# The high half of each weight times both halves of the activation in one 512-column matmul

## The reference, cut to what matters

```
def conv_ffn(h, w_in, conv_w, conv_b, w_out):
    u = h @ w_in
    u = causal depthwise convolution of u along the tokens (3 taps) + conv_b
    a, g = jnp.split(u, 2, axis=-1)
    return (a * jax.nn.gelu(g, approximate=True)) @ w_out

for layer in range(DEPTH):
    mod = (silu(c) @ ada_w[layer] + ada_b[layer])          # 6 sections: shift, scale, gate, twice
    h = rms_norm(x, ...) * (1.0 + sc_m) + sh_m
    x = x + g_m * rms_norm(mixer(h), ...)
    h = rms_norm(x, ...) * (1.0 + sc_f) + sh_f
    x = x + g_f * rms_norm(conv_ffn(h, ...), ...)
```

## The kernel before

| phase | layer 0: units, pieces per unit | layer 1 |
|---|---|---|
| gates | 1, 0 | 1, 0 |
| columns | 16, 1.5 | 16, 1.5 (side work: decays) |
| values (function `tokens`) | 8, 1 | 16, 0 (side work: GLA) |
| columns | 8, 2 (side work: fox) | 16, 0 (side work: GLA) |
| values | 8, 2 (fox) | |
| columns | 8, 1 (mLSTM) | |
| mixed (output projection) | 16, 1.5 | 16, 1.5 |
| ff_up / ff_down, group 0 | 32, 1 / 16, 1.5 | 32, 1 / 16, 0 |
| ff_up / ff_down, group 1 | 32, 1 / 16, 1.5 | 32, 0 / 16, 0 |
| ff_up / ff_down, group 2 | 24, 1 / 16, 0.5 | 24, 0 / 16, 0 |

## Time and profile before

### The profile page before, as it was taken

How to read it: one execution, slowest core, us unless ns; L and a number is a source line. 1 busy time by engine, 2 the same in 40 slices (tenths; PEclk the granted TensorE clock), 3 DMA queues, 4 the chain that set the end, 5 groups by cost and what they waited for, 6 DMA issues and landing times.

```text
span 2725.8 us, 48585 instructions
## 1 busy us (share of the span) xinstructions
PE 2538.6 (93%) x19382; PEld 2460.2 (90%) x19382; DVE 2017.8 (74%) x1998; ACT 1076.9 (40%) x1111; POOL 460.7 (17%) x230
## 2 busy tenths in 40 slices
PE   2599998989999999999989999989999999999997
PEld 2498877979999999999988989989899999999997
DVE  7876876789977799688777676667999456645655
ACT  1333334454433333233455544444533334333444
POOL 0100000013420244013301000000344014411320
PEclk7699989989999999999999999989999999999998
DMA  9887764747768767787665644357477455445543
GB/s 394 319 312 272 276 229 147 264 184 263 277 250 309 266 256 276 269 296 261 239 232 215 236 152 151 143 207 272 175 270 265 169 185 185 180 177 183 185 172 137
DMA packets 114640, 630.38 MB, mean 231 GB/s; under 512 B 12736, under 2 KB 12864, under 8 KB 62928
## 3 DMA queue, kind: packets, MB, share of 16 engines
q1 hardware_dynamic: 114512, 628.57, 63.0%
HBM read 626.42 MB, written 2.10 MB: 231 GB/s over the span
## 4 chain that ended last, share of the span: by engine, by line
PE 79%; DVE 9%; DMA 6%; ACT 3%; issue 2%; POOL 0%; DVEq 0%; SPq 0%; ACTq 0%; POOLq 0%
PE bank L1437 23%; PE bank L1438 22%; PE bank L1439 22%; DMA piece<-ada_pieces 4%; DVE acc L820 3%; PE bank L1456 2%; PE bank L1458 2%; PE bank L1457 2%; PE bank L1263 2%; DMA region<-ada_pieces 2%; DVE lo L806 1%; ACT hi L440 1%; PE bank L1341 1%; DVE act L865 1%; PE bank L1256 1%
## 5 line engine op out<-in xcount | busy, mean ns | idle before, releaser
L440 ACT ACTIVATE hi<-raw 128x2048 fp32r<-128x2048 f32 x402 | 769.6, 1915 | 1365.4 <-PE bank L1439 1238.0
L1437 PE MATMUL bank<-act,hi 128*128 128x256 f32 x4384 | 1266.8, 289 | 42.3 <-DVE act L865 26.1
L1438 PE MATMUL bank<-act,hi 128*128 128x256 f32 x4384 | 1252.7, 286 | 0.0
L1439 PE MATMUL bank<-act,lo 128*128 128x256 f32 x4384 | 1252.4, 286 | 0.0
L806 DVE TENSOR_TENSOR lo<-raw,hi 128x2048 fp32r<-128x2048 f32 x402 | 920.2, 2289 | 186.6 <-ACT hi L440 185.4
L1437 PEld LDWEIGHTS bank<-act,hi 128*128 128x128 f32 x4384 | 854.5, 195 | 52.6 <-issue 37.6
L1438 PEld LDWEIGHTS bank<-act,hi 128*128 128x128 f32 x4384 | 854.9, 195 | 1.0
L1439 PEld LDWEIGHTS bank<-act,lo 128*128 128x128 f32 x4384 | 854.0, 195 | 0.0
L820 DVE SCALAR_TENSOR_TENSOR acc<-piece,cond,acc 128x1024 f32<-128x1024 f32 x300 | 436.9, 1458 | 84.3 <-DMA piece<-ada_pieces 83.7
L1437 PE MATMUL bank<-mid,hi 128*128 128x256 f32 x1408 | 408.7, 290 | 12.3 <-POOL mid L790 11.2
L1438 PE MATMUL bank<-mid,hi 128*128 128x256 f32 x1408 | 402.2, 286 | 0.0
(11 more groups left out here) (155 smaller groups left out, 1612.0 us busy)
## 6 DMA issues: line engine op xcount, KB each, us to landing
raw<-w_units SPq DMA_DIRECT2D x402, 1024.0 KB, 4.8
piece<-ada_pieces SPq DMA_DIRECT2D x320, 512.0 KB, 4.9
region<-ada_pieces SPq DMA_DIRECT2D x64, 512.0 KB, 8.6
x<-x_in SPq DMA_DIRECT2D x1, 2048.0 KB, 15.0
x_out<-x SPq DMA_DIRECT2D x4, 512.0 KB, 2.6
vec<-vectors SPq DMA_DIRECT2D x1, 542.5 KB, 3.7
extra<-blocks_in SPq DMA_DIRECT2D x1, 512.0 KB, 18.9
causal<-causal_in SPq DMA_DIRECT2D x1, 256.0 KB, 18.1
```

Of the source, the lines that this page charges most:

```text
L440: sc.activation(hi[:, slot, :], raw[:, raw_slot, :], ACT.Copy).then_inc(s_hi, 1)
L1437: pe.matmul(dst, w_hi, src[:, kt, 0:T], start=at == 0, stop=False)
L1438: pe.matmul(dst, w_hi, src[:, kt, T:2 * T], start=False, stop=False)
L1439: i_ = pe.matmul(dst, w_lo, src[:, kt, 0:T], start=False, stop=at == len(order) - 1)
```

## The change

For each K tile the two matmuls with the same stationary operand `w_hi` become one of 512 columns, whose moving operand is the high and low half of the activation side by side. It writes a whole bank: columns 0:T hold high times high, columns T:2T weight-high times activation-low. The third matmul adds to columns 0:T as before. The two halves have to be added when the tile is taken out. VectorE can read one operand from PSUM, so ScalarE first copies columns T:2T into a new SBUF tile `low` (`stage_low`, with a semaphore `s_low`), and VectorE adds it. There is one `low`, so ScalarE also waits until the tile before has been taken out. In `ff_up` VectorE forms the sum in `low` and the convolution's three steps read it there; in `ff_down` groups 1 and 2 it adds `y` to `low` and then the tile. `stage_low` is the last thing in ScalarE's body of a unit, so it stands ahead of `hi` of the unit after next. The phases of kind `values` are as they were. `ones` shrinks to make room.

```diff
+            def stage_low(ph, i, j):
+                t = ph.t0 + j
+                sc.wait_ge(s_unit, SPLIT_SLOTS + unit(ph, i, j) + 1)
+                sc.wait_ge(s_evac, 2 + t + i * ph.tiles)
+                sc.activation(low[:, :], bank[2 * (t % 2)][:, T:2 * T], ACT.Copy).then_inc(s_low, 1)
...
                         if ph.sums and not (first_body(i) and j == 0):
                             square_tile(ph, ph.units * i + j - 1, (j + 1) % 2)
+                        if ph.kind != "values" and not (ph.side == "mlstm" and j == 3):
+                            stage_low(ph, i, j)
...
-                        if ph.kind != "values" or j % 4 == 3:
+                        if ph.kind != "values":
+                            ve.wait_ge(s_low, ph.c0 + i * ph.units + j + 1)
+                        elif j % 4 == 3:
                             ve.wait_ge(s_unit, SPLIT_SLOTS + n + 1)
...
                         elif ph.kind == "columns":
-                            ve.tensor_copy(region[:, bass.ds((ph.dest + ph.units * i + j) * T, T)], tile_ps)\
+                            ve.tensor_tensor(region[:, bass.ds((ph.dest + ph.units * i + j) * T, T)], tile_ps, low[:, :],
+                                             ALU.add).then_inc(s_evac, 1)
...
                         elif ph.kind == "ff_down":
                             at_ = flat(y[:, bass.ds(4 * i + j, 1), :])
-                            ve.tensor_tensor(at_, at_, tile_ps, ALU.add).then_inc(s_evac, 1)
+                            ve.tensor_tensor(low[:, :], at_, low[:, :], ALU.add).then_inc(s_v, own.tick())
+                            mine()
+                            ve.tensor_tensor(at_, tile_ps, low[:, :], ALU.add).then_inc(s_evac, 1)
...
-                            ve.tensor_scalar(out_, tile_ps, vec[:, bass.ds(ch + 2, 1)], vec[:, bass.ds(ch + 3, 1)],
+                            ve.tensor_tensor(low[:, :], tile_ps, low[:, :], ALU.add).then_inc(s_v, own.tick())
+                            mine()
+                            ve.tensor_scalar(out_, low[:, :], vec[:, bass.ds(ch + 2, 1)], vec[:, bass.ds(ch + 3, 1)],
                                              ALU.mult, ALU.add).then_inc(s_v, own.tick())
                             mine()
-                            ve.scalar_tensor_tensor(out=out_[:, 1:T], in0=tile_ps[:, 0:T - 1],
+                            ve.scalar_tensor_tensor(out=out_[:, 1:T], in0=low[:, 0:T - 1],
...
-                            ve.scalar_tensor_tensor(out=out_[:, 2:T], in0=tile_ps[:, 0:T - 2],
+                            ve.scalar_tensor_tensor(out=out_[:, 2:T], in0=low[:, 0:T - 2],
...
-                    dst = bank[2 * ((ph.t0 + j) % 2)][:, 0:T]
+                    both = bank[2 * ((ph.t0 + j) % 2)][:, :]
...
-                        pe.matmul(dst, w_hi, src[:, kt, 0:T], start=at == 0, stop=False)
-                        pe.matmul(dst, w_hi, src[:, kt, T:2 * T], start=False, stop=False)
-                        i_ = pe.matmul(dst, w_lo, src[:, kt, 0:T], start=False, stop=at == len(order) - 1)
+                        pe.matmul(both, w_hi, src[:, kt, :], start=at == 0, stop=False)
+                        i_ = pe.matmul(both[:, 0:T], w_lo, src[:, kt, 0:T], start=False, stop=at == len(order) - 1)
```

More of the change, by code:

```diff
@@ L68, in __init__, with place @@
         self.peel = self.head = 0
-    def place(self, n, t, a, pairs):
-        self.n0, self.t0, self.a0, self.pairs = n, t, a, pairs
+    def place(self, n, t, a, pairs, c):
+        self.n0, self.t0, self.a0, self.pairs, self.c0 = n, t, a, pairs, c
         self.end = n + self.bodies * self.units
@@ L75, in place @@
         pairs += 2 * self.bodies if self.kind == "ff_up" else 0
-        return self.end, t + self.bodies * self.tiles, self.a_end, pairs
+        c += 0 if self.kind == "values" else self.bodies * self.units
+        return self.end, t + self.bodies * self.tiles, self.a_end, pairs, c
     def straight(self, i):
@@ L111, in plan @@
               Phase("ff_up", 1, 6, 4, no, 2), Phase("ff_down", 1, 4, 4, no, 2)]
-    state = (0, 0, 2 * PIECES, 0)
+    state = (0, 0, 2 * PIECES, 0, 0)
     for ph in phases:
@@ L139 @@
 REGION = V_AT + TB * D
-OWN = {("ff_up", None): 8, ("columns", "fox"): 6, ("values", "fox"): 12, ("columns", "mlstm"): 14,
+OWN = {("ff_up", None): 12, ("columns", "fox"): 6, ("values", "fox"): 12, ("columns", "mlstm"): 14,
        ("values", "gla"): 8, ("columns", "gla"): 8}
@@ L223, in program @@
         ident = sb("ident", [P, P])
-        ones = sb("ones", [P, T])
+        ones = sb("ones", [P, P])
+        low = sb("low", [P, T])
         causal = sb("causal", [P, TB, T])
@@ L303, in program @@
         s_evac = sem("tile_evacuated")
+        s_low = sem("low_product_staged")
         s_piece = [sem(f"piece_ready{j}") for j in range(ADA_SLOTS)]
@@ L896, in gate_rows_ready @@
                 ve.wait_ge(s["masks_ready"], 1)
-                ve.tensor_tensor_scan(gate_rows, ones[0:GATES, :], gate_t2, 0.0, ALU.mult, ALU.add)\
+                ve.tensor_tensor_scan(gate_rows, ones[0:GATES, 0:1].broadcast_to([GATES, T]), gate_t2, 0.0, ALU.mult, ALU.add)\
                   .then_inc(s_v, own.tick())
@@ L1183, in body @@
                             bias = vec[0:GATES, V_GATEB:V_GATEB + 1] if ph.layer == 0 else 0.0
-                            ve.tensor_scalar(gates[:, :], tile_ps[0:GATES], bias, None, ALU.add).then_inc(s_evac, 1)
+                            ve.scalar_tensor_tensor(out=gates[:, :], in0=tile_ps[0:GATES], scalar=bias, in1=low[0:GATES, :],
+                                                    op0=ALU.add, op1=ALU.add).then_inc(s_evac, 1)
                         elif ph.kind == "columns":
-                            ve.tensor_copy(region[:, bass.ds((ph.dest + ph.units * i + j) * T, T)], tile_ps)\
+                            ve.tensor_tensor(region[:, bass.ds((ph.dest + ph.units * i + j) * T, T)], tile_ps, low[:, :],
+                                             ALU.add).then_inc(s_evac, 1)
+                        elif ph.kind == "mixed" or (ph.kind == "ff_down" and ph.group == 0):
+                            ve.tensor_tensor(flat(y[:, bass.ds(4 * i + j, 1), :]), tile_ps, low[:, :], ALU.add)\
                               .then_inc(s_evac, 1)
-                        elif ph.kind == "mixed" or (ph.kind == "ff_down" and ph.group == 0):
-                            ve.tensor_copy(flat(y[:, bass.ds(4 * i + j, 1), :]), tile_ps).then_inc(s_evac, 1)
                         elif ph.kind == "ff_down":
                             at_ = flat(y[:, bass.ds(4 * i + j, 1), :])
-                            ve.tensor_tensor(at_, at_, tile_ps, ALU.add).then_inc(s_evac, 1)
+                            ve.tensor_tensor(low[:, :], at_, low[:, :], ALU.add).then_inc(s_v, own.tick())
+                            mine()
+                            ve.tensor_tensor(at_, tile_ps, low[:, :], ALU.add).then_inc(s_evac, 1)
                         elif ph.kind == "ff_up":
@@ L1214, in body @@
                         k += ph.ada[j]
-                per = OWN.get((ph.kind, ph.side), 0)
+                per = ph.units if ph.kind == "ff_down" and ph.group > 0 else OWN.get((ph.kind, ph.side), 0)
                 roots_per = 2 if ph.side == "mlstm" else 0
```

## The result

| | before | changed |
|---|---|---|
| median, four executions each on one chip | 2718.97 us | 2742.78 us |
| lowest, highest | 2718.3, 2723.91 | 2730.93, 2745.96 |
| span of the profiled execution | 2725.8 us | 2744.2 us |
| mean granted clock | 0.958 | 0.950 |

The ratio is 1.0077 [1.0055, 1.0099]: slower by 0.8%, where 2701 was forecast and 2730 was the upper end of the range. A later repeat gave 1.0086 [1.0055, 1.0117].

What follows compares the result with a forecast made beforehand. TensorE was taken to bound the kernel, with VectorE 5% behind in 120 of 402 units. Terms -27.4 - 9 - 1 + 10 + 10.5, written as -17.9, took 2718.6 to 2701 us; range 2670 to 2730.

Steps and rivals of the forecast that it cites:

- the length of the chain in `ff_up`: VectorE's four evacuation steps per tile in `ff_up` with pieces, claimed to take 1.94 us.
- 5.86: Unit time in us for `ff_up` with pieces: 5.39 of VectorE work plus 0.47 given to GpSimd; +10 in all.
- the dearer evacuation: Rival: VectorE's evacuation in `ff_up` costs more, GpSimd's product hitting its SBUF-fed steps; 6.26 us per unit, 2747 us; chance 0.14.
- Phases where TensorE stays the bound, -27.4: Layer 1's `ff_up` and `ff_down`, `ff_down` group 2 and GLA's `columns` gain from the shorter matmuls, staging hidden: -27.4 us.
- The slack of 0.85: Where TensorE stays the bound, `hi` then `lo` end 4.7 us after a unit's end, weights wanted at 5.55.
- The merged matmul's 0.2266: Time in us per 512-column matmul, taken from `tokens`, against 0.2404 for two of 256 columns.
- Phases with three pieces in two units, -9: First `columns`, both `mixed` and layer 0's `ff_down` groups 0 and 1, 96 units: -9 us, against -20.6 at full rate.
- the limit by transfers: In layer 0's `ff_down` group 0, once the raw slots drain, piece DMAs set 12.1 us per pair of units.
- Ends of phases, +10.5: Staging and sum lengthen the last tile's path at phase changes, and the change of heads in GLA's `columns`: +10.5 us.
- GpSimd once per unit, 0.47: In `ff_up` with pieces VectorE gives GpSimd about 0.47 us once per unit, on the piece after `lo`.
- The five terms: TensorE-bound phases -27.4, three-piece phases -9, small chains (`fox`, `mlstm`, `gates`) -1, `ff_up` with pieces +10, phase ends +10.5.

Runs made afterwards that it cites:

- e3: The changed kernel with VectorE's `ff_up` bodies written out straight instead of looped; 2710.58 us, 0.9952 of the kernel before.
- e4: The changed kernel with the 16 wide matmuls of every tile issued first, then the 16 narrow ones; 2753.24 us, 1.0115 of the kernel before.
- e2: The changed kernel with the wide matmul but the old evacuation, leaving weight-high times activation-low out of the result; 2675.47 us, 0.984 of the kernel before.
- e6: e3 with the wide matmuls first in all but the first unit of a phase; 2702.60 us, 0.9946 of the kernel before.

## Why the prediction was wrong

**The step that failed** is the length of the chain in `ff_up`: "the chain is 0.46 + 0.43 + 0.52 + 0.53 = 1.94". In the loop it measures 0.60 + 0.56 + 0.63 + 0.73 = 2.52 beside a GpSimd step and 0.61 + 0.56 + 0.63 + 0.40 = 2.20 in the other unit. The rows it rested on were true and were the wrong unit. Without GpSimd the chain is 0.26 us longer than forecast; the other terms came out 0.12 shorter together, and 5.86 became 6.0. The forecast also took some 112 units as alike. By an estimate, 76 looped ones at 6.0 instead of 5.76 make +18, the straight ones stay under 5.76, and +18.0 was measured. e3 gives the control: with the gaps gone the chain is 0.45 + 0.45 + 0.52 + 0.40 = 1.82, the unit 5.71, the phases 719.3. So 1.94 was too long even for a straight unit, since the last step takes 0.40 to the next start and not 0.53: two errors of opposite sign, of which the loop's was the larger.

**The rival that came true** is the dearer evacuation, with 2747 given for 6.26 us per unit and 6.0 as the point from which it decides. The total came near its figure through other parts: the unit is 6.0, and the phases where TensorE was to stay the bound gave too little. Its reason, an extra price of the product on the new steps, holds only in part (below).

**Phases where TensorE stays the bound, -27.4.** In layer 1's `ff_up` without pieces -12.0 was expected and -2.1 came. VectorE has no piece there, but its chain of 2.2 us in gaps pushes `lo` back. Timelines of the changed kernel, VectorE and then GpSimd:

```profile
2285.86 2.83 DVE L819 TENSOR_TENSOR lo<-raw,hi 128x2048 fp32r<-128x2048 f32 x1
```

```profile
2285.81 0.73 POOL L803 TENSOR_TENSOR mid<-region,mid 128x256 f32 x1 [2.68 <-ACT mid L696]
```

The split of `mid` starts 0.05 us before `lo`, and `lo` takes 2.83 in place of 2.28. One unit in four then takes 6.05 to 6.2 us on TensorE, where the others take 5.55 to 5.75. The slack of 0.85 that the forecast worked out was for `lo` behind `hi`; it left out a GpSimd step in front of `lo`. In e3 the meeting is gone, and -9.4 of -12.0 came. In `ff_down` layer 1 groups 0 and 1 it is -1.9 for -6.8 + 1.8, since 0.3531 us per K tile gives 5.65 per unit and not 5.55. The merged matmul's 0.2266 was right (0.228 to 0.229 in the regular stream of e4); that a wide and a narrow one in turn need not add up to 0.3467 no row of before could show.

**Phases with three pieces in two units, -9.** Read by the table with 1.8 + 0.9 for their ends, -6.3 was due and -3.9, +0.1 and -1.7 came, -5.5. The sum is near, the reason is not: layer 0's first `columns` was to gain nothing and gained 4.2 us, and in `ff_down` group 0 of layer 0 the limit by transfers didn't appear. ScalarE's timeline of the changed kernel, `hi` in that phase (as the earlier trace rows):

```profile
809.00 1.91 ACT L443 ACTIVATE hi<-raw 128x2048 fp32r<-128x2048 f32 x1
...
893.88 1.91 ACT L443 ACTIVATE hi<-raw 128x2048 fp32r<-128x2048 f32 x1
```

These are 15 steps in 84.88 us, 5.66 each, to the end; before they fell to 6.07 after eight units. A slower `ff_up` ahead of it (199.2 for 194.4 us) leaves more in reserve, which would fit, but the repeat of the same kernel speaks against it. There `ff_up` took 200.0 us and the limit is back, in the phase that then takes 97.8 us:

```profile
880.84 1.91 ACT L443 ACTIVATE hi<-raw 128x2048 fp32r<-128x2048 f32 x1
...
893.09 1.91 ACT L443 ACTIVATE hi<-raw 128x2048 fp32r<-128x2048 f32 x1
```

These two units take 12.25 us, after seven of 5.68. In e2, where `ff_up` is faster (190.7), it is there too:

```profile
836.39 1.93 ACT L440 ACTIVATE hi<-raw 128x2048 fp32r<-128x2048 f32 x1 [4.95 <-PE bank L1438]
...
848.92 1.93 ACT L440 ACTIVATE hi<-raw 128x2048 fp32r<-128x2048 f32 x1 [4.97 <-PE bank L1438]
```

There two units take 12.53 us (836.39 to 848.92) after seven of 5.54, and the phase is 96.4 as before (96.5). e6 has `ff_up` at 192.6 and no limit (91.1). So the limit comes and goes between executions of one program, the first profile happened not to show it, and what brings it on is not settled.

**Ends of phases, +10.5.** This was the best part. Waits of the changed kernel:

```profile
PE bank L1458 <- POOL mid L803: 15.1, 4, 5.5
```

TensorE's wait for the last `mid` went from 11.2 to 15.1 us in the four places that this row holds. The first units of the six `ff_down` phases, from first matmul to first matmul, went from 7.11 to 8.29, 7.27 to 8.29, 9.37 to 10.42, 7.32 to 8.03, 7.05 to 7.72 and 9.40 to 10.22: +5.4 together, and 5.4 was said. The change of heads in GLA's `columns` went from 10.64 to 13.14 us, +2.5 for +2. That phase ends 4.1 us above before where -1.4 was due: its steps gave only 1.7 of 3.4, and its last unit, up to the first matmul of the next phase, went from 15.76 to 19.07, +3.3 us for which the forecast had no term. e3 and the repeat have the same 19.1; in e2, without staging and sum, it is 13.99.

**GpSimd once per unit, 0.47.** Of the size, right: the piece takes 1.76 beside it and 1.28 alone in the rows above. Wrong was that it always falls on the piece. In `ff_up` with pieces GpSimd was already running when the piece's sum started 108 times before, and 62 times in the changed kernel; 10 times it was `lo` (2.83 for 2.28, as above) and 36 times L1229, as at 1013.51 with 0.81 for 0.48. GpSimd's timeline:

```profile
1013.30 0.74 POOL L803 TENSOR_TENSOR mid<-region,mid 128x256 f32 x1 [2.58 <-ACT mid L696]
```

The Trainium skill (SBUF — State Buffer, the section "Who interferes with whom") says that a VectorE instruction with two SBUF inputs contends with a GpSimd instruction that reads SBUF. By the same page of the Trainium skill, section "SBUF: two separate sides", the one that starts first has the ports for its whole instruction. The trace agrees at all three places, with 0.33 to 0.55 us each. Whether the sum into `low`, which has one SBUF input, would have been spared no row of the changed kernel shows: none of its 176 ran beside a GpSimd instruction. How much of the loss is the exclusion and how much the loop's gaps was not tried apart: a kernel with GpSimd's steps shortened wasn't run.

**The sum.** The five terms add up to -16.9, not the -17.9 written; the forecast should have read 2702. e3's span lies 17.0 below before, which looks like that forecast without the loops' gaps. It is luck: with pieces it has -4.7 for +10, elsewhere it falls short by about as much, and the spans differ by 4 us more than the medians do (-13.0 against before on the same chip).

| us | forecast, ends of phases included | changed - before |
|---|---|---|
| start | 0 | +0.4 |
| `ff_up` with pieces | +10 | +18.0 |
| `ff_up` without | -12.0 | -2.1 |
| `ff_down` layer 1, groups 0, 1 | -5.0 | -1.9 |
| `ff_down` group 2 | -1.6 | +1.1 |
| GLA `columns` | -1.4 | +4.1 |
| three pieces in two units | -6.3 | -5.5 |
| gates, values, fox, mLSTM | -0.6 | +4.1 |
| sum | -16.9 | +18.2 (span +18.4) |

The last row but one is not clear of what executions differ by (405.1, 403.6 in the repeat, 399.0 in e3), and the lower granted clock in the fox `columns` goes with 2.7 us of it.

## What to carry to other kernels

Before you price a chain of dependent instructions on an engine, take its step from a unit in the steady loop, not from a prologue that happens to be written straight: here 0.04 against 0.15 to 0.19 us at three steps per unit was the difference between 0.5% faster (e3) and 0.8% slower. In a loop, look at the sequencer's rows too: here a register instruction between a wait and the step behind it is where the time went. A gain on the engine that sets the end is worth no more than the reserve of the next one, and that reserve is the unit's time less busy time less these gaps: 0.29 us by the straight unit, 0.16 or less by the loop's. When a change splits into a part that saves and a part that pays, run each alone early: -1.6% and +1.9% told at once that the evacuation was to be mended, not the matmul. And before you explain why a phase did or didn't hit a limit, look at a second execution of the same kernel.

## What the hardware did that was not expected

- The dependent steps of this chain on VectorE stand 0.04 us apart in all 52 straight units and 0.14 to 0.17, or 0.19 and more behind the first step, in all 124 looped ones, with durations unchanged. In the gap stands a register instruction of 0.06 or 0.10 us that carries the wait.
- A stream that alternates 512 and 256 columns keeps one of at least two steps, 0.347 or 0.353 us per pair, found at its start and kept until TensorE next stalls. Staging is not the reason, since e2, which has none, shows both. With the wide ones first it holds 5.57 us for 16 pairs.
- The `tensor_scalar` of 256 columns takes 0.413 us with two scalars from SBUF and an SBUF source, 0.54 from PSUM.
- A VectorE step of 0.48 us, shorter than GpSimd's own 0.74, is lengthened as well when GpSimd started first (L1229 at 1013.51).
